# The last sum of a mixture-of-experts step: three tiles summed by TensorE, the last pair's steps put in another order, and the final gain loaded early

## The reference

```
y = 0
for e in range(32):                                  # w: two experts of one group for each row
    a = silu(xt @ w_e_gate[e]) * (xt @ w_e_up[e])    # xt = rmsnorm(h), a: 256 wide
    y = y + combine[:, e:e+1] * (a @ w_e_down[e])    # combine is zero for 30 of the 32 experts
x = h + y
out = rmsnorm(x, final_norm_g)
```

## Time and profile before

| | us |
|---|---|
| median of three runs | 889.13 |
| the profiled execution, its own time | 890.63 |
| its span, first to last instruction | 888.8 |
| PE busy | 791.9 (89%) |
| DVE busy | 370.8 (42%) |
| ACT busy | 211.5 (24%) |
| POOL busy | 77.1 (9%) |

### The profile page before, as it was taken

The page is one execution under the profiler, slowest core; times in us unless marked ns, Lnnn a source line. Parts: engine busy times, 40 slices in busy tenths (PEclk is TensorE's granted clock), DMA queues, the critical chain, the costliest instruction groups (busy, mean ns, idle before and its releaser), DMA issues. The chain is left out here.

```text
span 888.8 us, 12013 instructions
## 1 busy us (share of the span) xinstructions
PE 791.9 (89%) x4643; PEld 581.8 (65%) x4643; DVE 370.8 (42%) x859; ACT 211.5 (24%) x388; POOL 77.1 (9%) x106
## 2 busy tenths in 40 slices
PE   5999999999999899999899998998999977777730
PEld 4887887779788666679899988997333332322210
DVE  2598466661700367448443248454211111110118
ACT  2320300001241344444433332112111110110003
POOL 0000230000111000000000000012011101001000
PEclk9999999999999999999999999997999999999975
DMA  9461273121436424310205334159899999999946
GB/s 364 161 204 48 72 87 109 48 94 55 173 139 221 187 76 162 130 61 1 95 24 204 140 130 185 48 230 422 344 418 420 419 421 421 419 420 420 419 122 262
DMA packets 33976, 186.12 MB, mean 209 GB/s; under 512 B 5915, under 2 KB 6187, under 8 KB 16808
## 3 DMA queue, kind: packets, MB, share of 16 engines
q1 hardware_dynamic: 21712, 146.63, 41.6%
q0 software_dynamic: 11344, 35.24, 12.4%
q10 hardware_dynamic: 864, 3.47, 1.0%
HBM read 176.17 MB, written 17.22 MB: 218 GB/s over the span
## 5 line engine op out<-in xcount | busy, mean ns | idle before, releaser
L479 PE MATMUL ps<-sb 128*128 128x288 f32 (+14 forms) x3038 | 592.2, 428 | 55.1 <-DMA sb<-in_wexp 31.6
L479 PEld LDWEIGHTS ps<-sb 128*128 128x128 f32 (+5 forms) x3038 | 386.9, 168 | 232.9 <-issue 145.9
L479 PE MATMUL ps<-sr 128*128 128x288 f32 (+1 forms) x1200 | 158.5, 292 | 1.6 <-DVE sr L1767 1.2
L479 PEld LDWEIGHTS ps<-sr 128*128 128x128 f32 x1200 | 155.1, 189 | 2.6 <-DVE sr L1767 1.4
L488 PEld LDWEIGHTS ps<-sb 128*128 128x128 f32 (+3 forms) x405 | 41.7, 140 | 35.5 <-issue 27.9
L2018 DVE SCALAR_TENSOR_TENSOR sb<-sb,ps 128x256 f32<-128x256 f32 x16 | 6.7, 421 | 125.7 <-ACT sb L1352 125.7
L488 PE MATMUL ps<-sb 128*128 128x128 f32 (+3 forms) x405 | 53.4, 270 | 5.0 <-DVEq L1846 2.0
L1767 DVE TENSOR_TENSOR sr<-sb,sr 128x2048 fp32r<-128x2048 f32 (+2 forms) x25 | 45.0, 1818 | 16.0 <-ACT sr L1239 12.8
L2026 DVE COPY sb<-ps 128x1024 f32<-128x1024 f32 x16 | 19.6, 1224 | 70.1 <-PE ps L479 70.1
L1057 ACT ACTIVATE sb<-ps 128x576 f32<-128x576 f32 (+4 forms) x29 | 22.9, 789 | 94.6 <-PE ps L479 66.9
L1755 DVE SCALAR_TENSOR_TENSOR sb<-sb,ps 128x576 f32<-128x576 f32 x24 | 18.0, 752 | 62.3 <-PE ps L479 62.3
(11 more groups left out here) (243 smaller groups left out, 435.6 us busy)
## 6 DMA issues: line engine op xcount, KB each, us to landing
sb<-in_wexp SPq DMA_DIRECT2D x96, 1024.0 KB, 27.4
sb<-in_wstream SPq DMA_DIRECT2D x34, 1024.0 KB, 4.9
sb<-in_mkT POOLq DMA_DIRECT2D x8, 512.0 KB, 7.1
sb<-in_mv POOLq DMA_DIRECT2D x8, 512.0 KB, 5.5
sb<-expert_rows SPq DMA_DIRECT2D x8, 512.0 KB, 9.3
sb<-in_xT ACTq DMA_DIRECT2D x4, 576.0 KB, 8.9
sb<-in_x SPq DMA_DIRECT2D x4, 512.0 KB, 7.3
sb<-k_pad POOLq DMA_DIRECT2D x8, 256.0 KB, 10.0
```

Of the source, the lines that this page charges most:

```text
L479: return signed(nc.tensor.matmul(*a, **kw))
```

## The change

On PE, `turn_hidden(15)` moves ahead of `down(14)`, and in front of it stand two products with the identity that put `h` of tile 4 in PSUM tile 0. Behind the expert stage PE gets new work: `h` of tile 2 goes to PSUM tile 2 once the last scatter has landed, `h` of tile 3 to PSUM tile 1 once the rows of tile 0 have landed, and then for tiles 2, 3 and 4 a product of a diagonal matrix (the weights `w0` on the diagonal) with the rows `y0` is added to it. DVE makes the three diagonals in pair 12. For tiles 2 to 4, DVE's first operation is gone, and its second reads PSUM in place of `h`. Its order is now combine 0, 1, finish 0, 1, combine 2, 3, finish 2, combine 4, finish 3, 4. The copy of pair 15's result is halved: DVE takes the first 512 columns, ACT the others. SP issues the gain's load behind the last weights. Some semaphores at the start of the program are merged; the same instructions wait for the same things there.

```diff
+R_DG = R_RH
+PE_TILES = {4: 0, 2: 2, 3: 1}
...
@@ sync
+            def load_gain():
+                sp.dma_start(at(M_GF, (1, D)), bass.AP(rows.tensor, rows.offset + D, [[0, P], [1, D]])).then_inc(ld["gf"], 16)
+
+            sp.wait_ge(xt_ps, NPAIR)
+            load_gain()
             with sp.If(overflow(sp) > 0):
...
             for s in range(2):
                 sp.wait_ge(y_sent[s], 16 * (NPAIR // 2))
-            sp.dma_start(at(M_GF, (1, D)), bass.AP(rows.tensor, rows.offset + D, [[0, P], [1, D]])).then_inc(ld["gf"], 16)
             for t in range(TT):
...
@@ tensor
+            def own_rows(t, start=True):
+
+                for half in range(2):
+                    mm(pat(PE_TILES[t], half * 512, (1, 512)), ident, at(O_H + t * D + half * 512, (1, 512)), start=start,
+                       stop=not start)
+
             def body(i, first, last):
...
                 if not last:
                     turn_rows(i + 1)
+                else:
+                    own_rows(4)
+                    turn_hidden(i)
                 if not first:
                     down(i - 1)
...
-                turn_hidden(i1 - 1)
                 down(i1 - 1)
...
+            pe.wait_ge(y_sent[1], 16 * (NPAIR // 2))
+            own_rows(2)
+            pe.wait_ge(ld_row[0], 48)
+            own_rows(3)
+            pe.wait_ge(diag_w, 1)
+            for t in (2, 3, 4):
+                pe.wait_ge(ld_row[t], 48 if t < TT - 1 else 64)
+                for half in range(2):
+                    last = mm(pat(PE_TILES[t], half * 512, (1, 512)), at(R_DG + (t - 2) * 128, (1, 128)),
+                              at(A_WG + t * 2048 + half * 512, (1, 512)), start=False, stop=True)
+                last.then_inc(more_ps, 1)
...
@@ scalar
             pairs(0, NPAIR)
+            act.wait_ge(y_ps, NPAIR)
+            act.wait_ge(y_sent[1], 16 * (NPAIR // 2 - 1))
+            fn(at(M_YO + 1536, (1, 512)), pat(3, 512, (1, 512)), ACT.Copy).then_inc(y_rest, 1)
...
@@ vector
-                v.tensor_copy(at(M_YO + (i % 2) * 1024, (1, 1024)), pat(3, 0, (1, 1024))).then_inc(y_copied, 1)
+                n = 512 if i == NPAIR - 1 else 1024
+                v.tensor_copy(at(M_YO + (i % 2) * 1024, (1, n)), pat(3, 0, (1, n))).then_inc(y_copied, 1)
+
+            def weight_diagonals():
+                for t in (2, 3, 4):
+                    c.do(v.tensor_scalar(at(R_DG + (t - 2) * 128, (1, 128)), ident, at(R_W0 + t, (1, 1)), None, ALU.mult))
+                c.settle()
+                dve.sem_inc(diag_w, 1)
...
-                op(v.scalar_tensor_tensor(h, at(A_WG + t * 2048, (1, D), pn=R), at(R_W0 + t, (1, 1), pn=R), h, ALU.mult, ALU.add))
-                c.do(v.scalar_tensor_tensor(h, at(A_WG + t * 2048 + D, (1, D), pn=R), at(R_W1 + t, (1, 1), pn=R), h,
+                if t not in PE_TILES:
+                    op(v.scalar_tensor_tensor(h, at(A_WG + t * 2048, (1, D), pn=R), at(R_W0 + t, (1, 1), pn=R), h, ALU.mult, ALU.add))
+                    rest = h
+                else:
+                    dve.wait_ge(more_ps, t - 1)
+                    rest = pat(PE_TILES[t], 0, (1, D), pn=R)
+                c.do(v.scalar_tensor_tensor(h, at(A_WG + t * 2048 + D, (1, D), pn=R), at(R_W1 + t, (1, 1), pn=R), rest,
...
@@ gpsimd
             def scatter(i):
                 pool.wait_ge(y_copied, i + 1)
+                if i == NPAIR - 1:
+                    pool.wait_ge(y_rest, 1)
```

More of the change, by code:

```diff
@@ L329, in build @@
         ssf, rootf, y_sum, y_done, y_st = (sem(n) for n in ("ssf", "rootf", "y_sum", "y_done", "y_st"))
+        more_ps, y_rest, diag_w = sem("more_ps"), sem("y_rest"), sem("diag_w")
         out_st = sem("out_st")
@@ L435, in _ @@
                     chunk(n, e)
+                sp.wait_ge(xt_ps, NPAIR_ALL)
+                load_gain()
                 for s in range(2):
@@ L567, in _ @@
                     owed.append((w_used, 1))
-            pe.wait_ge(y_built, 1)
+            pe.wait_ge(ssm_built, 1)
             for i in range(8):
@@ L576, in _ @@
                 last.then_inc(ps_ready, 1)
-            pe.wait_ge(vt_built, 1)
+            pe.wait_ge(ssm_built, 2)
             for i in range(4):
@@ L1018, in _ @@
             with pe.If(overflow(pe) > 0):
+                own_rows(4, start=False)
                 pe.wait_ge(oh2_ready, 1)
@@ L1039, in _ @@
             act.wait_ge(ld["small"], 16)
-            fn(at(O_SM + S_T, (1, 32)), at(O_SM + S_LD, (1, 32)), ACT.Exp).then_inc(exp_ssm, 1)
+            fn(at(O_SM + S_T, (1, 32)), at(O_SM + S_LD, (1, 32)), ACT.Exp).then_inc(ssm_act, 1)
             act.wait_ge(ang_ready, 1)
-            fn(at(O_SM + S_T + 32, (1, 32)), at(O_SM + S_T + 64, (1, 32)), ACT.Exp).then_inc(exp_ssm, 1)
-            fn(at(O_SM + S_T + 96, (1, 64)), at(O_SM + S_T + 160, (1, 64)), ACT.Sin).then_inc(trig, 1)
-            act.wait_ge(ones_set, 2)
+            fn(at(O_SM + S_T + 32, (1, 32)), at(O_SM + S_T + 64, (1, 32)), ACT.Exp).then_inc(ssm_act, 1)
+            fn(at(O_SM + S_T + 96, (1, 64)), at(O_SM + S_T + 160, (1, 64)), ACT.Sin).then_inc(ssm_act, 1)
+            act.wait_ge(consts_set, 2)
             for t in range(TT):
@@ L1391, in op @@
                     c.settle()
-            v.memset(at(O_RS, (1, 16)), 1.0).then_inc(ones_set, 1)
-            dve.wait_ge(ones_set, 1)
+            v.memset(at(O_RS, (1, 16)), 1.0).then_inc(consts_set, 1)
+            dve.wait_ge(consts_set, 1)
             op(v.memset(at(O_EPS, (1, 1)), EPS))
-            v.memset(at(O_ONE, (1, 128)), 1.0).then_inc(ones_set, 1)
-            v.memset(at(A_ZERO, (1, 112)), 0.0).then_inc(zero_set, 1)
+            v.memset(at(O_ONE, (1, 128)), 1.0).then_inc(consts_set, 1)
+            v.memset(at(A_ZERO, (1, 112)), 0.0).then_inc(consts_set, 1)
             dve.wait_ge(ld["small"], 16)
@@ L1426, in _ @@
             dve.sem_inc(diag_ready, 1)
-            dve.wait_ge(exp_ssm, 2)
-            dve.wait_ge(trig, 1)
+            dve.wait_ge(ssm_act, 3)
             pr, pi = O_PW, O_PW + 288
@@ L1513, in _ @@
                 if hf:
-                    c.do(ins, y_built)
+                    c.do(ins, ssm_built)
                 else:
@@ L1528, in _ @@
                 if hf:
-                    c.do(ins, vt_built)
+                    c.do(ins, ssm_built)
                 else:
@@ L2032, in pairs @@
                         result(i - 1)
+                    if i == NPAIR - 4:
+                        weight_diagonals()
                 result(i1 - 1)
@@ L2054, in _ @@
                 pairs(NPAIR, NPAIR_ALL)
+                dve.wait_ge(ld["gf"], 32)
             c = main
@@ L2076, in _ @@
             combine(0)
-            for t in range(TT):
-                if t + 1 < TT:
-                    combine(t + 1)
-                finish(t)
+            combine(1)
+            finish(0)
+            finish(1)
+            combine(2)
+            combine(3)
+            finish(2)
+            combine(4)
+            finish(3)
+            finish(4)
         @block.gpsimd
@@ L2089, in store @@
                 stores[0] += 1
-            pool.wait_ge(zero_set, 1)
+            pool.wait_ge(consts_set, 3)
             pool.dma_start(k_d[:, :, 0:112].rearrange("(a g) h c -> (g h) a c", g=8),
@@ L2208, in _ @@
                 pool.wait_ge(idx_ready, 3)
+                pool.wait_ge(ld["gf"], 16)
                 pairs(NPAIR, NPAIR_ALL)
```

8 lines of the change are left out of this document (4 added, 4 removed).

## The result

The changed kernel takes 883.02 us (median of 6 runs, 882.05 to 883.93), the kernel before, in runs beside it, 889.34 us (886.56 to 890.07): 6.3 us less, ratio 0.9932, 95% interval 0.9917 to 0.9947. The forecast was 882.7. The profiled execution took 882.53 us, its span is 880.7.

The account below looks back on a forecast made before the run. Bounds: PE's weight wait around the last pair, no computing from last scatter to first combine, then gapless DVE. Terms -1.70-0.55-2.0-3.2+1.0 = -6.45 us gave 882.7 us from the 889.13 median; range 880.6 to 885.8.

Parts of the forecast that it names:

- load: From SyncE's first row issue behind the last scatter to DVE's first operation; forecast 2.0 us shorter.
- last stage: DVE's first to last operation: -3.2 us for three operations gone, +1.0 (0 to +3.6) for waiting on PE.
- The gap and the clock: PE's idle 2.21 us before `down(14)`: filled, the clock stays 2.4 GHz and `down(14)` takes 3.65 us, -1.70.
- Rival 4: Median executions lack the slow `down(14)`, so its -1.70 us is worth nothing there: 884.4 us; chance 10%.
- The move of the transposes: `turn_hidden(15)` ahead of `down(14)` gives nothing alone, as `down(15)` waits for DVE's later copy of result 14.
- The halved copy: Pair 15's result copied half by DVE, half by ACT, in place of 1.23 us on DVE: -0.55 us.
- The gain's load: Gain loaded behind the last weights, no longer ahead of the final rows: -2.0 us.
- the bound of 2.4: Upper bound in us on what moving the gain's load saves: 0.4 issue plus 2.0 DMA time.
- Rival 3: Tile 0's rows are slow regardless of the gain; only its issue is saved, -0.4 us: 884.3 us; chance 12%.
- Rival 1: PE at 2.4 GHz throughout the last stage, so the +1.0 us falls away: 881.7 us; chance 20%.
- Rival 2: PE at 1.2 GHz throughout the last stage and the bound, +3.6 us for +1.0: 885.3 us; chance 10%.
- Rival 5: PE stays at 1.2 GHz from pair 15 on, making the kernel slower, +5.5 us: 894.7 us; chance 3%.

Follow-up runs that it names:

- e8: Kernel before plus two unused identity products in the gap ahead of `down(14)`; 887.14 us beside 888.77, ratio 0.9988 (0.9973 to 1.0003).
- e9: Kernel before, profiled a second time without any edit; 889.74 us in one run.
- e3: Changed kernel with `turn_hidden(15)` behind `down(14)` again, `h` products staying in the gap; 883.82 us, ratio 0.9952 to the kernel before.
- e4: Changed kernel with the last result copied whole by DVE, nothing by ACT; 883.56 us, ratio 0.9952 to the kernel before.
- e10: Changed kernel with tile 3's `h` product done twice, at the landings of tile 0's and tile 1's rows; 883.5 us, ratio 0.9932.
- e1: Changed kernel with the gain's load issued behind the last scatter again, in front of the rows; 884.76 us, ratio 0.9958 to the kernel before.
- e6: Changed kernel with the `h` products of tiles 2 and 3 directly behind `down(15)`, without their waits; 883.59 us beside 883.66 for the changed kernel.
- e7: Changed kernel with `h` products of tiles 2 and 3 repeated to no effect, keeping PE at work behind `down(15)`; 883.67 us.
- e2: Changed kernel with tile 4's two `h` products moved from the gap to behind `down(15)`; 884.45 us beside 888.94 for the kernel before, ratio 0.9959.
- e11: Changed kernel with tile 2's `h` product done three times behind the scatter's landing; 882.85 us beside 888.77 for the kernel before, ratio 0.9937.

## Why the prediction was right, step by step

From the start of `gate_up(15, 1)`, means of the two profiles of each kernel, in us:

| step | forecast | measured |
|---|---|---|
| `down(14)` | -1.70 | -1.70 |
| from its end to `down(15)` | 0 | +0.1 |
| end of `down(15)` to scatter issue | -0.55 | -0.53 |
| scatter issue to SyncE's next | 0 | +0.3 |
| load | -2.0 | -2.7 |
| last stage | -3.2 + 1.0 | -1.9 |
| sum | -6.45 | -6.4 |

*The gap and the clock.* The step is there as argued: filled by useless products alone (e8), `down(14)` takes 3.65 us, and so it does in each of the twelve profiles with the gap filled or split. Rival 4, that the median's executions lack the slow `down(14)`, is weakened by e9, which has it again, but not out: two profiles are not the median, e8's runs leave both open, and behind other gaps of 2 us the clock fell only in 6 of 27 cases. The count that the rival gave was a misreading: in the trace of the kernel before, the clock fell five times before 857 us (near 305, 602, 622, 779 and 844 us), not three. That two products cost nothing, because `down(14)` waits for its weights, held to 0.1 us.

*The move of the transposes.* Nothing, for the named reason (e3): the copy of result 14 is still there. With the move, the last weights are named as last in its place, at 0.1 us.

*The halved copy.* -0.53 (e4). But the scatter then took 3.2 us to land in place of 2.9. It did so in e4 too, where the copy is whole, so the copy is not the cause; it was 2.8 in e10. What it is stays open.

*The gain's load.* This term was mis-sized: -2.0. Against two profiles each it measures -2.7, beyond the bound of 2.4; over all profiles, 4 with the gain late have a load of 7.4 on average (6.93 to 7.70), 10 with it early 5.0, which is the bound. I had taken the transfer's 2.0 us and let the issue run beside it; they add up. From the first issue of the rows it is 7.0 us with the gain ahead and 5.0 without, which is the transfer, and the gain's own issue stands 0.38 us in front of that. Rival 3, only the issue saved, is out by e1's load; e1's runs stand only about 1 us above their neighbours, so the size in the median stays open. By the rule on the ports in the Trainium skill (SBUF — State Buffer, Door 1: The DMA port swizzle) this term would have been 1.3, further off from the profiles.

*The last stage.* -1.9 for -2.2. I had one tile's product at 1.2 GHz, tile 2's, and it was this one: in each of the two profiles the clock fell around the end of the idle time between tile 3's `h` and tile 2's rows (3.3 and 4.0 us) and was back by the first third of tile 3's product at the latest. The forecast had DVE wait 0.7 us for tile 2 and about 0.5 for tile 3; it waited 0.64 and 0.61, in the second profile 0.64 and 0.44. That it would be just one tile was a choice between readings, and so partly luck. Rival 1, full clock through the `h` products' warmth, is out: the clock fell in both profiles, and the waits that were to prevent it make no difference (e6). Its price is confirmed, 16.64 us in e7. Rival 2 is out as well: no stretch at 1.2 GHz outlasted the weighted products, and tile 4's ran at full clock in each profile that has it. PSUM as an operand: I took 1.25 us with the gaps from a row of another line; it is 1.27 to 1.28, as from SBUF, neither the saving of that row nor the loss of the table in the Trainium skill (VectorE: DVE Perf Modes, The TRN2 errata). The second profile of the changed kernel was 0.5 us slower here, as combine 1 waited 0.71 us for tile 1's rows.

*Rival 5*, slower, never came near: the clock stayed at 2.4 GHz through both `down` groups in all twelve.

That the sum fits to 0.1 us is luck in part: -0.7 on the load stands against +0.3 on the scatter and +0.3 on the last stage.

## What to carry to other kernels

Read the last wait at each step before crediting a move: here the transposes were hidden behind a copy, and what paid there was that added work filled an idle gap ahead of matmuls, which then ran at full clock. Count how often the clock falls at such gaps before pricing one: two profiles of a kernel are few. A load that needs nothing late goes behind the last bulk transfer; in front of the final loads it costs its issue and its transfer. And when TensorE takes work from a stage that has been without it, its clock is part of the price: ask what it did in the microseconds before.

## What the runs showed of the hardware

- The granted clock fell behind idle gaps of 2.21 and 2.09 us of PE ahead of `down(14)`, and not in the one profile in which the gap was split by 0.4 us of transposes (e2). At two other places of the expert stage gaps of 1.8 to 2.3 us were followed by a fall in 6 of 27 cases. In the last stage it fell near the end of gaps of 3.3 and 4.0 us, 0.3 us behind the start of the products in one profile and 0.3 us before it in the other. Most falls lasted 3.4 us, but one 10.1 in e10 with PE busy 7.94 of them.
- TensorE reading SBUF without a pause at 1.2 GHz did not slow the loading of tile 0's rows: it took 4.79 us (e11); without such work 4.66 to 5.07. At 2.4 GHz (e7) the later rows landed 512 KB in 1.23 to 1.29 us, as in e11, but tile 0's were 1.1 us late, for a reason that is not known.
- One of SyncE's ten issues for the rows took 1.5, 1.8 and 1.6 us in e7, e8 and e9, against 0.43 to 0.88 in the others. In e7 it came behind both issues for tile 0, so it doesn't explain that execution's late first operation.
